# Access patterns of the large matmuls varied by chunk number: a weight step of two, runs from two halves, eight places

## The reference

```python
def swiglu(h, w13, w2):
    a, b = jnp.split(h @ w13, 2, axis=-1)
    return (jax.nn.silu(a) * b) @ w2
...
for l in range(DEPTH):
    y = swiglu(modulate(x, ...), ffn_w13[l, 0], ffn_w2[l, 0])
    x = layer_norm(ALPHA * x + 0.5 * (1 + mod[:, 0, 2])[:, None, :] * y, ln_g[l, 0], ln_b[l, 0])
    y = token_mixer(modulate(x, ...), w_in[l], w_out[l], ...)
    ...
    y = swiglu(modulate(x, ...), ffn_w13[l, 1], ffn_w2[l, 1])
```

## Time and profile before

| | us |
|---|---|
| median of 2 runs | 2118.69 |
| lowest and highest | 2117.75 and 2119.63 |
| the profiled execution's own time | 2114.09 |
| its span, first to last instruction | 2111.9 |

### The profile page before, as it was taken

The page is one execution under the profiler, slowest core; times in us unless marked ns, Lnnn a source line. Parts: engine busy times, 40 slices in busy tenths (PEclk is TensorE's granted clock), DMA queues, the critical chain, the costliest instruction groups (busy, mean ns, idle before and its releaser), DMA issues.

```text
span 2111.9 us, 39270 instructions
## 1 busy us (share of the span) xinstructions
PE 2015.4 (95%) x16744; PEld 1860.8 (88%) x16744; DVE 1576.4 (75%) x2135; ACT 1071.8 (51%) x1516; POOL 307.9 (15%) x247
## 2 busy tenths in 40 slices
PE   7999989999999999899999999898999997989998
PEld 7999879979988998789889989787899887979996
DVE  6688788776987676688675649886788489758874
ACT  4544365455434443564554435565665375656652
POOL 0200022111000200203011003610120036002100
PEclk9999999999999999999999999999999999999999
DMA  9888743335985677443245663233455534324552
GB/s 376 333 312 330 268 160 131 110 120 201 358 343 193 242 282 296 148 162 122 81 172 207 249 220 117 105 141 109 151 201 189 197 128 146 121 100 160 205 196 79
DMA packets 60381, 409.85 MB, mean 194 GB/s; under 512 B 6896, under 2 KB 6896, under 8 KB 13872
## 3 DMA queue, kind: packets, MB, share of 16 engines
q1 hardware_dynamic: 54000, 384.85, 49.5%
q0 software_dynamic: 5920, 22.07, 3.1%
q10 hardware_dynamic: 288, 0.42, 0.1%
HBM read 404.17 MB, written 3.15 MB: 193 GB/s over the span
## 4 chain that ended last, share of the span: by engine, by line
PE 75%; DVE 14%; ACT 4%; DMA 2%; issue 2%; POOL 2%; SPq 0%; DVEq 0%; POOLq 0%; ACTq 0%
PE ps L719 13%; PE ps L721 13%; PE ps L720 13%; PE ps L763 7%; PE ps L764 7%; PE ps L765 7%; DVE l L607 4%; DMA w<-in_stream 2%; PE ps L1731 2%; PE ps L748 2%; PE ps L750 2%; PE ps L749 2%; PE ps L631 1%; DVE tmp L981 1%; ACT h L592 1%
## 5 line engine op out<-in xcount | busy, mean ns | idle before, releaser
L607 DVE TENSOR_TENSOR l<-w,h 128x2048 fp32r<-128x2048 f32 (+1 forms) x295 | 672.4, 2282 | 157.3 <-ACT h L592 157.1
L719 PE MATMUL ps<-xh,h 128*128 128x256 f32 x2544 | 727.0, 286 | 17.4 <-DVE gq L2429 8.2
L592 ACT CAST h<-w 128x2048 fp32r<-128x2048 f32 (+1 forms) x295 | 556.1, 1890 | 344.0 <-PE ps L765 174.6
L720 PE MATMUL ps<-xl,h 128*128 128x256 f32 x2544 | 717.7, 282 | 0.0
L721 PE MATMUL ps<-xh,l 128*128 128x256 f32 x2544 | 716.6, 282 | 0.0
L719 PEld LDWEIGHTS ps<-xh,h 128*128 128x128 f32 x2544 | 483.0, 190 | 25.7 <-DVE l L607 11.6
L720 PEld LDWEIGHTS ps<-xl,h 128*128 128x128 f32 x2544 | 483.2, 190 | 2.4 <-issue 2.4
L721 PEld LDWEIGHTS ps<-xh,l 128*128 128x128 f32 x2544 | 484.5, 190 | 0.0
L763 PE MATMUL ps<-h,hh 128*128 128x512 f32 x528 | 209.9, 398 | 0.0
L764 PE MATMUL ps<-l,hh 128*128 128x512 f32 x528 | 208.3, 394 | 0.0
L765 PE MATMUL ps<-h,hl 128*128 128x512 f32 x528 | 208.2, 394 | 0.0
(11 more groups left out here) (425 smaller groups left out, 3003.7 us busy)
## 6 DMA issues: line engine op xcount, KB each, us to landing
w<-in_stream SPq DMA_DIRECT2D x361, 1024.0 KB, 4.9
GB<-in_vec POOLq DMA_DIRECT2D x20, 512.0 KB, 5.9
w<-in_stream SPq DMA_DIRECT2D x8, 512.0 KB, 4.2
gate<-in_vec POOLq DMA_DIRECT2D x6, 512.0 KB, 3.9
memf<-in_memT SPq DMA_DIRECT2D x2, 512.0 KB, 6.2
xf<-in_xT POOLq DMA_DIRECT2D x1, 1024.0 KB, 8.7
kv<-mk POOLq DMA_DIRECT2D x2, 512.0 KB, 6.5
kv<-mv POOLq DMA_DIRECT2D x2, 512.0 KB, 9.1
```

Source lines behind the costliest of these rows:

```text
L592: e.copy(place_in(k.H, m, z), k.W[n % NW][:, 0:z]).then_inc(k.hi_done, 1)
L607: e.tensor_tensor(place_in(k.L, m, z), k.W[n % NW][:, 0:z], place_in(k.H, m, z), SUB).then_inc(k.lo_done, 1)
L719: p.matmul(P[:, 0:T], H[:, r, o], xh[:, r, :], start=r == 0, stop=False)
L720: p.matmul(P[:, 0:T], H[:, r, o], xl[:, r, :], start=False, stop=False)
```

## The change

The new function `run_of` picks a number for each chunk from its position: `FIRST[c] // 8 % 4`, so eight chunks in a row share it and after 32 chunks it comes round again. The numbers are 128 (plain), 16, 8 and 4. The place counts modulo eight now, so all four patterns go through all eight places.

- Chunks with features on the partitions. Run 16 or 8: the streamed tokens are read in runs of that many, in turn from the first and the second half of the 256, and the results are written to PSUM in the same order, so each token's result stands where it stood. Run 4: the tokens are read plainly, and the weight tile is read with a step of two floats; `stored` has interleaved the two tiles' columns for that.
- Chunks with tokens on the partitions, and DOWN chunks. The streamed H or L is read in runs of 16, 8 or 4, in turn from the two halves of the 256 or 512 columns; `stored` has put the columns so that the results come out in the order of before.

An opening chunk has its tokens read plainly whatever its number; a weight step of two applies there too. `pack` shuffles the columns on the host before the launch. What is computed stays the same.

The lists of instructions of the two kernels, engine by engine, with their operands' tiles and their waits, are the same in number and in order: 12268 rows on TensorE, and no difference on VectorE, ScalarE, GpSimd and SyncE. Only the shapes of matmuls on TensorE differ. How many of them have which pattern:

| chunks | plain | 16 | 8 | 4 |
|---|---|---|---|---|
| features, 256 columns, 48 matmuls each | 41 | 46 | 48 | 35 |
| tokens, 256 columns, 48 matmuls each | 11 | 4 | 6 | 13 |
| DOWN, 24 matmuls of 512 columns each | 26 | 19 | 17 | 24 |
| 128 columns (four of features with 24 matmuls, two of tokens with 48) | 6 | | | |

Of the 46 and 48 feature chunks with runs, three and two are opening chunks, so 43 and 46 of them (2064 and 2208 matmuls) stream in runs.

```diff
@@ -125,6 +125,33 @@
 
 def width(c):
     return len(MIXCOLS[c[2]][1]) if c[0] == "win" else 256
+
+
+def features(c):
+
+    k = c[0]
+    return k in ("w13", "wup") or (k == "win" and MIXCOLS[c[2]][0] == "fm") or (k == "win2" and (c[2] < 6 or c[2] >= 16)) or (k == "wkv" and c[2] < 2)
+
+
+def run_of(c):
+
+    if c[0] in DOWN or width(c) == 256:
+        return (128, 16, 8, 4)[FIRST[c] // 8 % 4]
+    return 128
+
+
+def stored(c):
+
+    g = run_of(c)
+    if features(c):
+        n = width(c)
+        return [x % 2 * 128 + x // 2 for x in range(n)] if g == 4 else list(range(n))
+    n = D if c[0] in DOWN else width(c)
+    if g == 128:
+        return list(range(n))
+    z = 512 if c[0] in DOWN else n
+    half = [x % (z // 2) // g * 2 * g + x // (z // 2) * g + x % g for x in range(z)]
+    return [y + x for y in range(0, n, z) for x in half]
 
 
 def pack(inp):
@@ -160,6 +187,9 @@
             w = km(inp["w_up_2"][c[1]][:, c[2] * FF + c[3] * 256:c[2] * FF + c[3] * 256 + 256])
         else:
             w = km(inp["w_down_2"][c[1]][c[2] * 256:c[2] * 256 + 256])
+        if k != "ada":
+            at = stored(c)
+            w = w.reshape(128, -1, len(at))[:, :, at].reshape(128, -1)
         S[n, :, :w.shape[1]] = w
     return S
 
@@ -549,7 +579,7 @@
 
 def place_in(b, m, z=CH, first=0):
 
-    o = 8 * (m % 16)
+    o = 8 * (m % 8)
     return b[m % NH][:, o + first:o + z]
 
 
@@ -698,6 +728,24 @@
         v = lambda b: rr(place_in(b, m, 8 * n), "p (k n) -> p k n", k=rows)
         return v(k.H), v(k.L)
 
+    def tile_of(self, B, r, j):
+
+        if run_of(MATS[self.m - 1]) == 4:
+            return rr(B[:, r, :], "p (t j) -> p j t", j=2)[:, j]
+        return B[:, r, j * 128:j * 128 + 128]
+
+    def tokens_of(self, v):
+
+        g = run_of(MATS[self.m - 1])
+        return rr(v, "p (h t e) -> p t h e", h=2, e=g) if g in (8, 16) else v
+
+    def stream(self, m, B, r, z, x=0):
+
+        c = MATS[m]
+        g = run_of(c) if c[0] in DOWN or z == 256 else 128
+        v = B[:, r, x * z:x * z + z]
+        return v if g == 128 else rr(v, "p (h t e) -> p t h e", h=2, e=g)
+
     def bank(self):
         k, t = self.k, self.t
         self.t += 1
@@ -712,13 +760,14 @@
 
         k, p = self.k, self.p
         P = self.bank()
-        o = slice(j * 128, j * 128 + 128)
         for r in range(8):
             for w in ready[r] if ready else ():
                 p.wait_ge(*w)
-            p.matmul(P[:, 0:T], H[:, r, o], xh[:, r, :], start=r == 0, stop=False)
-            p.matmul(P[:, 0:T], H[:, r, o], xl[:, r, :], start=False, stop=False)
-            i = p.matmul(P[:, 0:T], L[:, r, o], xh[:, r, :], start=False, stop=r == 7)
+            h, l = self.tile_of(H, r, j), self.tile_of(L, r, j)
+            y, a, b = (self.tokens_of(v) for v in (P[:, 0:T], xh[:, r, :], xl[:, r, :]))
+            p.matmul(y, h, a, start=r == 0, stop=False)
+            p.matmul(y, h, b, start=False, stop=False)
+            i = p.matmul(y, l, a, start=False, stop=r == 7)
         i.then_inc(k.tile_pe, 1)
 
     def opening(self, H, L, n, xh, xl, ready):
@@ -727,15 +776,15 @@
         P = [self.bank() for j in range(n)]
         for part in range(2):
             for j in range(n):
-                o = slice(j * 128, j * 128 + 128)
                 for r in range(8):
                     if j == 0:
                         p.wait_ge(*ready[part](r))
+                    h, l = self.tile_of(H, r, j), self.tile_of(L, r, j)
                     if part == 0:
-                        p.matmul(P[j][:, 0:T], H[:, r, o], xh[:, r, :], start=r == 0, stop=False)
-                        p.matmul(P[j][:, 0:T], L[:, r, o], xh[:, r, :], start=False, stop=False)
+                        p.matmul(P[j][:, 0:T], h, xh[:, r, :], start=r == 0, stop=False)
+                        p.matmul(P[j][:, 0:T], l, xh[:, r, :], start=False, stop=False)
                     else:
-                        i = p.matmul(P[j][:, 0:T], H[:, r, o], xl[:, r, :], start=False, stop=r == 7)
+                        i = p.matmul(P[j][:, 0:T], h, xl[:, r, :], start=False, stop=r == 7)
                 if part:
                     i.then_inc(k.tile_pe, 1)
 
@@ -745,24 +794,25 @@
         P = self.bank()
         o = slice(a * 128, a * 128 + 128)
         for r in range(8):
-            p.matmul(P[:, 0:n], xh[:, r, o], H[:, r, :], start=r == 0, stop=False)
-            p.matmul(P[:, 0:n], xh[:, r, o], L[:, r, :], start=False, stop=False)
-            i = p.matmul(P[:, 0:n], xl[:, r, o], H[:, r, :], start=False, stop=r == 7)
+            h, l = self.stream(self.m - 1, H, r, n), self.stream(self.m - 1, L, r, n)
+            p.matmul(P[:, 0:n], xh[:, r, o], h, start=r == 0, stop=False)
+            p.matmul(P[:, 0:n], xh[:, r, o], l, start=False, stop=False)
+            i = p.matmul(P[:, 0:n], xl[:, r, o], h, start=False, stop=r == 7)
         i.then_inc(k.tile_pe, 1)
 
-    def down_bank(self, H, L, ks, a, n, banks, hh, hl, ready, first, last):
+    def down_bank(self, m, H, L, ks, a, n, banks, hh, hl, ready, first, last):
 
         k, p = self.k, self.p
         o = slice(a * 128, a * 128 + 128)
         P = k.ps[banks[2 * a + n]]
-        s = slice(n * 512, n * 512 + 512)
         for i, f in enumerate(ks):
             if ready is not None:
                 p.wait_ge(*ready(f))
             b, e = first and i == 0, last and i == 1
-            p.matmul(P[:, :], hh[:, f, o], H[:, i, s], start=b, stop=False)
-            p.matmul(P[:, :], hh[:, f, o], L[:, i, s], start=False, stop=False)
-            x = p.matmul(P[:, :], hl[:, f, o], H[:, i, s], start=False, stop=e)
+            h, l = self.stream(m, H, i, 512, n), self.stream(m, L, i, 512, n)
+            p.matmul(P[:, :], hh[:, f, o], h, start=b, stop=False)
+            p.matmul(P[:, :], hh[:, f, o], l, start=False, stop=False)
+            x = p.matmul(P[:, :], hl[:, f, o], h, start=False, stop=e)
         return x
 
 
@@ -786,7 +836,7 @@
                 p.wait_ge(*k.freed[b])
     for a in range(2):
         for n in range(2):
-            x = pe.down_bank(H, L, keys[c], a, n, banks, hh, hl, ready if a + n == 0 else None, c == 0, False)
+            x = pe.down_bank(pe.m - 1, H, L, keys[c], a, n, banks, hh, hl, ready if a + n == 0 else None, c == 0, False)
     x.then_inc(k.down_pe, 1)
     pe_ada(k, p, pe.m - 1)
 
@@ -802,7 +852,7 @@
             for c, (H, L) in zip(cs, got):
                 if a and h and c == n - 1 and not again:
                     pe_turn(k, p, s, 0)
-                x = pe.down_bank(H, L, keys[c], a, h, banks, hh, hl, None if a or h else ready, False, c == n - 1)
+                x = pe.down_bank(pe.m - n + c, H, L, keys[c], a, h, banks, hh, hl, None if a or h else ready, False, c == n - 1)
                 if a + h == 2 or c == n - 1:
                     x.then_inc(k.down_pe, 1)
     if again:
```

## The result

The changed kernel takes 2154.5 us (median of 2 runs, 2153.33 and 2155.67) against 2118.69 us. The ratio is 1.0169, 95% interval 1.0125 to 1.0213: slower by 36 us. That is clear of no change; whether it is more than 2% isn't. I had forecast 2101.5 us, so the sign was wrong. The time lies above the forecast's own range (2084 to 2119), though inside the wider one given for 8 in 10 (2076 to 2225). The profiled execution is one of the two, 2155.67 us, 41.6 us above that of before.

A forecast was written before the change was run, and what follows sets the result against it. The prediction took TensorE's matmul pace as the bound. Half of 7.7 + 24.7 + 8.4 us is 20.4 us, times 0.85 is 17 us, from 2114.1 to 2097, or 2101.5 us on the median's scale; range 2084 to 2119.

The forecast's parts named there:

- What bounds the kernel: TensorE's matmul pace sets the time; 0.85 of any change of pace is passed on to the span.
- Part 1: Places counted modulo 8 instead of 16 move some chunks by 256 bytes; cost 0.
- full gain: Every changed matmul reaching the best pace seen, 113.6 ns for 256 columns, 227.1 for 512; 40.8 us before passing on.
- Part 2: Weight loads with a step of two in 1680 feature matmuls; half of a 7.7 us gain counted.
- rival with a slow load: Step of two slows feature weight loads, up to double duration, 2288 us; decides from 27 ns more per load; chance 0.14.
- Part 3: Runs in streamed tokens, weights and PSUM writes; half of gains of 24.7 us (256 columns) and 8.4 us (512) counted.
- Why a gain at all: Argument that runs or stepped loads give stream and load equal speed modulo 256 bytes, so they can stay clear; half counted.
- meetings: Weight read and streamed read supposedly colliding in memory, depending on their address distance modulo 256 bytes, which slows matmuls.
- rival on breaks: Each break between runs in the stream costs 0.43 ns; 105 us passed on, 2223 us; chance 0.15, from half the price.
- Nothing changes: Rival: collisions of the two reads are only shared out anew among places and chunks; 2119 us, chance 0.22.
- all meetings vanish: Rival: every collision of the two reads in changed matmuls goes; 35 us gained, 2084 us, chance 0.13.

The follow-up runs named there:

- e1_places: Changed kernel with every pattern made plain, places modulo 8 kept; 2117.07 us against 2118.08 for the kernel before, ratio 0.9999.
- e7_place0: Kernel before, all patterns plain, with every chunk put at place 0; 2103.92 us against 2115.29, ratio 0.9945.
- e4_sides: Changed kernel with feature reads and PSUM writes in runs separated, all runs in skipping order (even runs, then odd); DOWN runs of 16, 8, 4: 240, 232, 233 ns.
- e6_distance: Changed kernel, all chunks at place 0, streaming single words from two blocks 2 to 128 floats apart, or plain; DOWN mostly 216 ns from 4 floats up.
- e11_steps: Changed kernel with streams at constant steps of 2, 4, 16 floats or skipping pairs; whole kernel 3520 us, sampled DOWN chunks 433 to 460 ns.
- e12_lanes: Changed kernel, features plain, streamed weights word by word from stepped halves, quarters or eighths; DOWN halves with step two 227 ns, step four 453, quarters 280.

## Why the prediction was wrong

- *What bounds the kernel*: right. The pace of the matmuls is the bound, and 0.91 of the change in pace was passed on between the profiled executions, 0.78 between the medians, for the 0.85 of the sum.
- *Part 1, places modulo 8, cost 0*: right (e1_places, ratio 0.9999). Reading the places as a distance between two addresses modulo 256 bytes was right too in DOWN chunks (e7_place0). For the feature side it was half right: the 113.6 ns that set the full gain there isn't a matter of the place alone.
- *Part 2, the step of two*: I took a gain of 2.3 ns a matmul, half of 4.6. It costs 1.7. The rival with a slow load was further off: 2 ns and not 27 or more. (It counted the 27 ns in the pace; with 6 ns of slack the load itself would have had to be 33 ns longer.)
- *Part 3, the runs*: this is the step that failed. I took half of a full gain, (24.7 + 8.4) / 2 = 16.6 us. Measured on those matmuls was a loss of 43 us. The argument under "Why a gain at all" treated the pace as 6% that can't be had and a remainder from meetings that patterns could remove. In runs taken in turn the pace doesn't fall toward 227 ns; it settles at 240, 243 and 252. In runs of 16 and 8 it is nearly the same at all places, so the spread by place did go, as equal speeds would have it, but at a price above the worst plain place; in runs of 4 even the spread stayed (247 to 257). The sum weighed only the lapping of two readers. What the order of the words costs in the stream itself stood at nothing in it, and only the rival on breaks gave it a price.
- *The rival on breaks* had the right place and sign. Its price was 0.43 ns per break; counted that way the measured one is 0.25, 0.18 and 0.16 ns per break for DOWN runs of 16, 8 and 4, and 0.12 and 0.16 on the feature side. But it isn't a price per break: e4_sides has as many breaks at 232 and 233 ns for runs of 8 and 4 in skipping order. What runs in turn cost beyond plain ones, 8 to 20 ns on 512 columns, stays unexplained by any experiment here; the rule of the two sides puts them in the plain class. A load of weights ran beside every stream measured, so whether a stream alone would have these paces isn't known.
- *Nothing changes* and *all meetings vanish* are out by the paces above.
- *The page on SBUF lines* (the Trainium skill, "SBUF — State Buffer", section "Door 1: The DMA port swizzle") made runs of four and a step of two free, as the prediction worked out. The line of 16 bytes is borne out by e6_distance (227 ns at 8 bytes, 216 at 16). Two accesses to a line as the condition for full speed are not: a step of two in the stream has two in a row and took 454 ns in e11_steps, a plain stream has four and loses 6%. In the load the step of two cost 2 ns.
- *The page on PSUM lines* (the Trainium skill, "Advanced Engine Details and Errata", section "PSUM Cachelines") says both that any access in pieces is slow and that pairs are enough. The first doesn't hold here and the second does: writes in runs of 8 and of 2 kept the plain 118 ns (e4_sides).

## What to carry to other kernels

When TensorE is the bound, read the distance between starts and compare it with columns over clock: the mean duration of a matmul hides a 6 to 12% loss that the order of the streamed words decides. Storing a float32 operand as two halves and streaming them word by word in turn removes nearly all of that loss (227 to 237 down to 216 ns for 512 columns) at no cost at run time if the operand is laid out beforehand, while a constant step or pairs over many lines double the time. Where a kernel doesn't yet use it, a small probe that gives each chunk another pattern and is read chunk by chunk, as this change can be, tells more than one timed variant.

## What the runs showed of the hardware

The pace of a 512-column fp32r matmul, by how the words in even and in odd position of the stream use the 16-byte lines. This is a rule that fits the patterns tried, found after the fact for all but e12_lanes; the mechanism behind it was not seen, and it gives the order of the classes, not their times.

| each side (even, odd) takes | patterns | ns |
|---|---|---|
| all four words of a line in a row | single words in turn, distance 4 floats or more | 216 |
| two | plain; runs of 64 in turn; distance 2; skipping runs of 8 or 4; halves with a step of two | 227 to 237 |
| two, runs in turn, or skipping runs of 16 | runs of 32, 16, 8, 4 | 236, 240, 243, 252 |
| one, but back on that line after one other | quarters; runs of 2 in turn | 280, 330 |
| one, and on to the next | steps of 2, 4, 16; skipping pairs; halves with a step of four | 433 to 461 |
| one, back after three others | eighths | 487 |

For 256 columns the fastest pattern gives 112 ns and not 216 / 2 = 108. That is also the pace of a chunk with 128 columns, which points to the load of the weights as the bound there; no run changed the load under such a stream.
